# FFN gate and up: one 512-column product for both parts of x, halves added on VectorE, and GpSimd scaling x one instruction per tile

## The chip, the cores and the metric

The kernel runs on one core of one Trainium2 chip, as one launch. The metric is the device time of that launch in microseconds, the median of several runs. Each core has five engines that run their own instruction streams and meet at semaphores: TensorE (PE, matrix products; its weight loads are shown as PEld), VectorE (DVE), ScalarE (ACT), GpSimd (POOL), and SyncE (SP), which here issues the loads. A product reads a stationary operand of 128x128 and a moving one of up to 512 columns, and writes up to one PSUM bank (128 x 512 fp32). There are eight banks.

## The reference, cut to what matters

Two transformer blocks follow one another on 256 tokens of width 1024. The first has attention, retention, a memory attention and a mixture of 32 experts. The second has two layers, each with two feed-forward networks (FFN) around a mixer, so four FFN in all. Everything is fp32. The part that the change works on is this:

```python
D_MODEL = 1024; SEQ = 256; D_FF = 2816; DEPTH_2 = 2
def _swiglu(h, w_gu, w_down):
    gate, up = jnp.split(h @ w_gu, 2, axis=-1)
    return (jax.nn.silu(gate) * up) @ w_down
...
for l in range(DEPTH_2):
    x = _layer_norm(alpha * x + 0.5 * _swiglu(x, ffn_w_gu[l, 0], ffn_w_down[l, 0]), ln_g[l, 0], ln_b[l, 0])
    mix = _token_mixers(x, ...)
    x = _layer_norm(alpha * x + mix, ln_g[l, 1], ln_b[l, 1])
    x = _layer_norm(alpha * x + 0.5 * _swiglu(x, ffn_w_gu[l, 1], ffn_w_down[l, 1]), ln_g[l, 2], ln_b[l, 2])
```

`_layer_norm` ends in `* g + b`; that scaling of x is what GpSimd does in `pool_affine`. The first block's attention has 8 heads (`ATTN_HEADS`) and 4 retention heads.

## The kernel before, in words

**Split operands.** Products run in the rounded format fp32r. To keep fp32 accuracy, each operand is split in a high part (the rounded value) and a low part (the rest), and a product a*b becomes three: high*high, high*low, low*high. For the FFN, `whu` and `wlu` are the high and low part of a tile's gate and up weights, `whd` and `wld` those of its down weights, `xh` and `xl` those of x transposed (8 blocks `k` of 128 features by 256 tokens), `hh` and `hl` those of the hidden values.

**Tiles.** An FFN (numbered `g`, 0 to 3) has `FT` = 22 tiles `t` of 128 hidden units. Buffers alternate by `p` = t mod 2. For each tile PE does `up(t, p)` (L1031): for the two halves `m` (0 gate, 1 up) and the eight blocks `k`, three products of 256 columns, (`whu`,`xh`), (`whu`,`xl`), (`wlu`,`xh`), into columns `m*256` on of bank 4+p. Then `down(t, p)` (L1072): 12 products of 512 columns into banks 0 to 3, which hold the sum over all tiles. The order on PE is written out: `up_first()` (tile 0, L1050, the products with `xl` last, since `xl` comes later), then a loop of 20 rounds `up(t+1)`, `down(t)`, then `up(21)`, and at the end `down_into` (L1057) for tiles 20 and 21 by banks: nine products of tile 20, a wait for the hidden values of tile 21 (`f_h`), then three products for each bank of tile 21.

**The other engines.** ACT: `silu(t)` (L1106) reads the gate half of the bank into `sg`, then waits for the end of `down(t-1)` and makes `whd(t+1)` and `whu(t+2)` (`ffn_high`, L928). DVE: `hidden(t)` multiplies `sg` with the up half of the bank into `hf` (L1158), rounds it into `hh` (L1160) and subtracts for `hl` (L1162, which signals `f_h`); then `low(t+1)` and `low(t+2)` subtract for `wld(t+1)` and `wlu(t+2)` (`ffn_low`, L933, which counts up `wl_ok`). SP streams 1.5 MB per tile into a ring.

**GpSimd in an FFN.** `pool_affine` scales x with `ln`: four multiplications of 128x512 (L976), then four additions (L981). In FFN 1, 2 and 3 it starts when `wl_ok` shows that `wld` of tile 1 is made, and runs through. Its end (`xp_ok`) is waited for only before the next `ln` is loaded and in the norm after the FFN.

**The end of an FFN.** After `silu(21)` ACT makes the high part of the next stage's weights (L512, or L928 for the next FFN), POOL the low part (L521, or L939), then POOL the inverse root of the norm (L566), ACT scales x (L1214, L1215), and PE transposes (L1010).

**The attention of the first block** (about 97 to 134 us). `pe_units` walks over the 8 heads `u`. The table `AHEAD1` says in which step the scores (L1965) of which heads are computed: heads 0 and 1 in step 0, 2 and 3 in step 1, 4 and 5 in step 3, 6 and 7 in step 5. Head v's scores lie in bank v mod 2, so they wait until DVE has taken the logits of head v-2 (`lg_ok`). Between them stand retention scores (L2099) and values (L2110), transposes of probabilities (L1975) and attention values (L1984). DVE makes the logits (L2055) and their maxima (L2059) one head ahead, and the norm of retention (L2527, L2530, L2536, with POOL's L2120, L566 in between).

## Time and profile before

| | us |
|---|---|
| median of 3 runs | 1827.29 |
| lowest, highest run | 1823.26, 1829.07 |
| the profiled execution | 1831.82 |
| its span, first to last instruction | 1830.0 |
| PE busy in the span | 1645.0 (90%) |
| DVE busy | 853.7 (47%) |
| ACT busy | 639.8 (35%) |
| POOL busy | 262.6 (14%) |
| four FFN, about | 736 to 920, 1085 to 1268, 1281 to 1467, 1631 to 1819 |
| experts, about | 290 to 735 |

A row of the chain of work gives start, length, what ran and how many instructions. A matmul's recorded length includes its way through the array: the pace is the distance between starts, not the length. "waited for" and "idle before" name what released an engine.

### The profile page before, as it was taken

The page shows a single profiled execution, that of the slowest core. Times are in us where ns is not written, and L with a number is a line of the kernel's source. Part 1 is how long each engine was busy: PE and PEld are TensorE (multiplying, and loading weights), DVE is VectorE, ACT ScalarE, POOL GpSimd, SP SyncE. Part 2 cuts the span into 40 slices and gives each one's busy share as a digit, 9 for nine tenths or more (in the row PEclk, how much of TensorE's full clock was granted, in tenths as well). Part 3 has the DMA queues.
Part 4 walks back from the last instruction along what each step waited for, and adds up shares of the span by engine and source line. Part 5 has one row for each costly group of instructions (what it writes and reads, how often), then busy time and mean ns, then how long its engine had stood idle before and what let it go on. Part 6 is the DMA issues. An engine that isn't in the chain of part 4 may idle for free.

```text
span 1830.0 us, 29586 instructions
## 1 busy us (share of the span) xinstructions
PE 1645.0 (90%) x11837; PEld 1310.8 (72%) x11837; DVE 853.7 (47%) x1290; ACT 639.8 (35%) x948; POOL 262.6 (14%) x253
## 2 busy tenths in 40 slices
PE   8989999777766776999999899999999999899997
PEld 6777885333323332999977779998999977779996
DVE  4574443111110111555555655555655565666555
ACT  5445442100010011333433644444333333644442
POOL 1233210000000000100143422001300143431000
PEclk9989999977788887999999999999999999999999
DMA  9514578999999999945533054536454543055501
GB/s 393 171 38 138 195 283 334 425 426 427 426 426 426 425 426 407 358 176 188 198 138 138 24 198 180 185 124 236 176 194 180 187 149 124 24 207 182 196 35 46
DMA packets 60949, 421.38 MB, mean 230 GB/s; under 512 B 7008, under 2 KB 16064, under 8 KB 17216
## 3 DMA queue, kind: packets, MB, share of 16 engines
q1 hardware_dynamic: 59136, 409.13, 57.0%
q10 hardware_dynamic: 1728, 11.03, 1.7%
q8 instruction: 64, 1.05, 0.2%
q14 instruction: 21, 0.17, 0.0%
HBM read 419.08 MB, written 1.05 MB: 230 GB/s over the span
## 4 chain that ended last, share of the span: by engine, by line
PE 63%; DMA 10%; SPq 9%; DVE 5%; ACT 5%; POOL 4%; issue 4%; DVEq 0%; ACTq 0%; POOLq 0%
PE bank L1031 26%; PE bank L1072 12%; SPq L1683 9%; PE bank L1820 6%; PE bank L1771 5%; DMA ring<-in_we 4%; DMA more<-in_we 4%; PE bank L1846 2%; PE bank L650 2%; DMA ring<-in_wf 1%; PE bank L1984 1%; POOL small L566 1%; PE bank L1050 1%; PE bank L1965 1%; POOL wlu L939 1%
## 5 line engine op out<-in xcount | busy, mean ns | idle before, releaser
L1031 PE MATMUL bank<-xh,wlu 128*128 128x256 f32 x1344 | 379.9, 283 | 0.0
L1031 PE MATMUL bank<-xh,whu 128*128 128x256 f32 x1344 | 379.8, 283 | 0.0
L1031 PE MATMUL bank<-xl,whu 128*128 128x256 f32 x1344 | 379.8, 283 | 0.0
L1031 PEld LDWEIGHTS bank<-xh,whu 128*128 128x128 f32 x1344 | 257.0, 191 | 3.3
L1031 PEld LDWEIGHTS bank<-xl,whu 128*128 128x128 f32 x1344 | 256.9, 191 | 3.3
L1031 PEld LDWEIGHTS bank<-xh,wlu 128*128 128x128 f32 x1344 | 257.2, 191 | 0.0
L933 DVE TENSOR_TENSOR wlu<-ring,whu 128x2048 fp32r<-128x2048 f32 x84 | 196.3, 2337 | 51.2 <-ACT whu L928 51.2
L933 DVE TENSOR_TENSOR wld<-ring,whd 128x1024 fp32r<-128x1024 f32 x88 | 110.0, 1250 | 188.6 <-ACT whd L928 188.6
L928 ACT ACTIVATE whu<-ring 128x2048 fp32r (+1 forms) x88 | 167.2, 1902 | 3.5 <-DMA ring<-in_wf 3.5
L928 ACT ACTIVATE whd<-ring 128x1024 fp32r (+1 forms) x88 | 93.3, 1060 | 206.1 <-PE bank L1072 202.6
L650 PE MATMUL bank<-ring,xg 128*32 128x256 f32 x1424 | 104.0, 430 | 40.6 <-DMA ring<-in_we 40.6
L1820 PE MATMUL bank<-ring_r,xTh 128*128 128x512 f32 x384 | 112.9, 407 | 9.9 <-POOL ring_r L490 6.0
L1106 ACT ACTIVATE sg<-bank 128x256 f32<-128x256 f32 x88 | 33.8, 384 | 228.5 <-PE bank L1031 210.0
L939 POOL TENSOR_TENSOR wlu<-ring,whu 128x512 fp32r<-128x512 f32 x16 | 20.1, 1287 | 648.8 <-ACT whu L928 614.3
L650 PEld LDWEIGHTS bank<-ring,xg 128*32 128x32 f32 x1424 | 43.9, 119 | 96.1 <-DMA ring<-in_we 68.6
L669 PE MATMUL bank<-ring,hTe 128*32 128x256 f32 x832 | 75.6, 499 | 36.0 <-DMA ring<-in_we 27.6
L829 DVE TENSOR_TENSOR hmid<-hact,bank 128x128 f32<-128x128 f32 x32 | 9.2, 288 | 199.9 <-ACT hact L717 199.9
L1072 PE MATMUL bank<-whd,hl 128*128 128x512 f32 x320 | 100.9, 397 | 0.0
L1072 PE MATMUL bank<-whd,hh 128*128 128x512 f32 x320 | 100.5, 395 | 0.0
L1072 PE MATMUL bank<-wld,hh 128*128 128x512 f32 x320 | 100.4, 394 | 0.0
L1820 PEld LDWEIGHTS bank<-ring_r,xTh 128*128 128x128 f32 x384 | 73.5, 194 | 28.7 <-issue 8.8
L521 POOL TENSOR_TENSOR ring_r<-ring,high 128x512 fp32r<-128x512 f32 x32 | 41.3, 1322 | 349.2 <-ACT high L512 349.0
(317 smaller groups left out, 2745.6 us busy)
## 6 DMA issues: line engine op xcount, KB each, us to landing
ring<-in_we SPq DMA_DIRECT2D x141, 1024.0 KB, 26.8
ring<-in_wf SPq DMA_DIRECT2D x88, 1536.0 KB, 6.8
ring<-in_w SPq DMA_DIRECT2D x52, 1024.0 KB, 4.9
more<-in_we SPq DMA_DIRECT2D x51, 1024.0 KB, 25.7
ring<-in_w SPq DMA_DIRECT2D x32, 256.0 KB, 3.4
ln<-in_ln ACTq DMA_DIRECT2D x6, 1024.0 KB, 4.9
bias<-in_bias ACTq DMA_DIRECT2D x2, 2048.0 KB, 8.1
bias<-in_bias SPq DMA_DIRECT2D x1, 2048.0 KB, 20.1
```

The costliest lines, as they stand in the source:

```text
L521: ins = eng.tensor_tensor(slot_r[s][:, part], slot[s][:, part], run.highs[c % 2][:, part].bitcast(F32), ALU.subtract)
L650: ins = pe.matmul(bank[4 + e % 2][q * CAP:(q + 1) * CAP, 0:2 * P], xg[:, k, e * CAP:(e + 1) * CAP], w[:, kk, q], start=(k == 0), stop=(k = ...
L669: ins = pe.matmul(bank[6][q * CAP:(q + 1) * CAP, 0:2 * P], hTe[:, e % 2, k * CAP:(k + 1) * CAP], w[:, kk, q], start=(k == 0), stop=(k == 3 ...
L928: act.activation(dst[:], ring[:, bass.ds(ring_tile(t) + first, D if down else 2 * D)], ACT.Copy).then_inc(wh_ok, 1)
L933: eng.tensor_tensor(dst[:], ring[:, bass.ds(ring_tile(t) + first, D if down else 2 * D)], src[:].bitcast(F32), ALU.subtract).then_inc(done, 1)
L939: ins = eng.tensor_tensor(wlu[p][:, c0:c0 + 512], ring[:, ring_tile(t) + c0:ring_tile(t) + c0 + 512], whu[p][:, c0:c0 + 512].bitcast(F32), ...
L1031: ins = pe.matmul(bank[4 + p][:, m * S:(m + 1) * S], w[p][:, cols], v[:, k], start=(k == 0 and n == 0), stop=(k == KD - 1 and n == 2))
L1072: ins = pe.matmul(bank[2 * i + c][:], v[p][:, tok(i)], w[p][:, c * 512:(c + 1) * 512], start=False, stop=False, skip_group_check=True)
L1683: sp.dma_start(slot[s], src).then_inc(e_land[s], 16)
L1771: ins = pe.matmul(bank[sel + 2 * i + c0 // 512][:, 0:c1 - c0], v[:, k, tok(i)], w[:, kk, c0:c1], start=(k == 0 and m == 0), stop=(k == KD ...
L1820: ins = pe.matmul(bank[banks[2 * i + h]][:], v[:, k, tok(i)], w[:, kk, h * 512:(h + 1) * 512], start=(k == 0 and m == 0), stop=(k == KD - ...
L1846: ins = pe.matmul(bank[b][:, i * MD:(i + 1) * MD], v[:, k, tok(i)], w[:, k], start=(k == 0 and m == 0), stop=(k == KD - 1 and m == 2))
```

## The change

**Products.** `xh` and `xl` become the two halves of one tile `xhl`. In `up`, the two products with `whu` become one of 512 columns whose moving operand is `xhl[:, :, k]`, two runs of 256 columns that lie 2048 elements apart. The product with `wlu` stays at 256 columns and adds into the first half. Gate now has a bank of its own (4 + 2p) and up another (5 + 2p); in each bank the first half holds the products with `xh`, the second that with `xl`. `up_first` keeps 48 products of 256 columns, with `xl` into the second half.

**Halves.** `hidden` begins with two `tensor_reduce` instructions on DVE, which read a whole bank and add the halves: gate into `sg` (signals `f_ga`), up into `hf`. ACT's `silu` waits for `f_ga` in place of `f_gu` and works on `sg` in place; the multiplication reads `sg` and `hf`, both in SBUF.

**GpSimd.** In FFN 1 to 3 `pool_affine` starts one count of `wl_ok` later (`wlu` of tile 2 is made) and then waits two counts, that is one tile, before each further instruction.

**Attention.** `AHEAD1` now computes the scores of one head per step: after heads 0 and 1 in step 0, head u+1 in step u.

```diff
-        xh = at("xh", work + 12288, [P, KD, S], F32R)
-        xl = at("xl", work + 20480, [P, KD, S], F32R)
+        xhl = at("xhl", work + 12288, [P, 2, KD, S], F32R)
+        xh, xl = xhl[:, 0], xhl[:, 1]
...
-        AHEAD1 = {0: (0, 1), 1: (2, 3), 3: (4, 5), 5: (6, 7)}
+        AHEAD1 = {0: (0, 1), **{u: (u + 1,) for u in range(1, AH - 1)}}
...
-        def pool_affine(pool, st, j, after):
-
-            pool.wait_ge(*after)
+        def pool_affine(pool, st, j, after, step=0):
+
+            sem_at, first = after
+            pool.wait_ge(sem_at, first)
...
+            for n in range(8):
+                i, c = n // 2 % 2, n % 2
+                cols = slice(c * 512, (c + 1) * 512)
+                if n == 4:
+                    st.sync()
+                if n and step:
+                    pool.wait_ge(sem_at, first + n * step)
+                ins = pool.tensor_tensor(x[:, i, cols], x[:, i, cols], ln[:, n // 4, cols], (ALU.mult, ALU.add)[n // 4])
+                if n < 7:
+                    st.then(ins)
...
-                        for n, (w, v) in enumerate(((whu, xh), (whu, xl), (wlu, xh))):
-                            ins = pe.matmul(bank[4 + p][:, m * S:(m + 1) * S], w[p][:, cols], v[:, k],
-                                            start=(k == 0 and n == 0), stop=(k == KD - 1 and n == 2))
+                        into = bank[4 + 2 * p + m]
+                        pe.matmul(into[:].rearrange("p (a s) -> p a s", a=2), whu[p][:, cols], xhl[:, :, k],
+                                  start=(k == 0), stop=False, skip_group_check=True)
+                        ins = pe.matmul(into[:, 0:S], wlu[p][:, cols], xh[:, k],
+                                        start=False, stop=(k == KD - 1), skip_group_check=True)
...
+                        if g == 0 and m == 1 and not low_x:
+                            pe.wait_ge(t_out, tb + 2)
...
-                act.wait_ge(f_gu, t + (g * FT + 1))
-                act.activation(sg[:, p], bank[4 + p][:, 0:S], ACT.Silu).then_inc(f_sg, 1)
+                act.wait_ge(f_ga, t + (g * FT + 1))
+                act.activation(sg[:, p], sg[:, p], ACT.Silu).then_inc(f_sg, 1)
...
+                gate, upper = bank[4 + 2 * p], bank[5 + 2 * p]
+                dve.wait_ge(f_gu, t + (g * FT + 1))
+                dve.tensor_reduce(sg[:, p], gate[:].rearrange("p (a s) -> p s a", a=2), X, ALU.add).then_inc(f_ga, 1)
+                dve.tensor_reduce(hf[:, p], upper[:].rearrange("p (a s) -> p s a", a=2), X, ALU.add).then_inc(f_hv, 1)
                 dve.wait_ge(f_sg, t + (g * FT + 1))
-                dve.tensor_tensor(hf[:, p], sg[:, p], bank[4 + p][:, S:2 * S], ALU.mult).then_inc(f_hv, 1)
-                dve.wait_ge(f_hv, t * 2 + (g * FT * 2 + 1))
+                dve.wait_ge(f_hv, t * 3 + (g * FT * 3 + 1))
+                dve.tensor_tensor(hf[:, p], sg[:, p], hf[:, p], ALU.mult).then_inc(f_hv, 1)
...
-                    pool_affine(pool, st, l * 3 - 1, (wl_ok, (g + 1) * FFN_W + 4))
+                    pool_affine(pool, st, l * 3 - 1, (wl_ok, (g + 1) * FFN_W + 5), 2)
...
-                pool_affine(pool, st, l * 3 + 1, (wl_ok, (g + 1) * FFN_W + 4))
+                pool_affine(pool, st, l * 3 + 1, (wl_ok, (g + 1) * FFN_W + 5), 2)
```

The order of instructions at two places. First PE in the attention of the first block, in steps 3 and 4: L1965 (after: L1975) are scores, with bank0 for an even head and bank1 for an odd one, L2110 (L2120) retention values, L1984 (L1994) attention values, L1975 (L1985) transposes, L2099 (L2109) retention scores. Before:

```order
L1975 MATMUL bank2<-ident_53,lg1_143 128x128 x4
L1965 MATMUL bank0<-qkT_94 128x256
L1965 MATMUL bank1<-qkT_94 128x256
L1965 MATMUL bank0<-qkT_94 128x256
L1965 MATMUL bank1<-qkT_94 128x256
L2110 MATMUL bank7<-proj_92,xT_51 128x128 x4
L1984 MATMUL bank4<-proj_92,xT_51 128x64 x4
L1975 MATMUL bank3<-ident_53,lg1_143 128x128 x4
L2099 MATMUL bank6<-qkT_94 128x256 x2
```

The same place of PE with the change:

```order
L1985 MATMUL bank2<-ident_53,lg1_142 128x128 x4
L1975 MATMUL bank0<-qkT_94 128x256 x2
L2120 MATMUL bank7<-proj_92,xT_51 128x128 x4
L1994 MATMUL bank4<-proj_92,xT_51 128x64 x4
L1985 MATMUL bank3<-ident_53,lg1_142 128x128 x4
L1975 MATMUL bank1<-qkT_94 128x256 x2
L2109 MATMUL bank6<-qkT_94 128x256 x2
```

Head 4's two score products now stand alone before the retention values, and head 5's have moved behind the next transposes, ahead of the retention scores.

Second, DVE at the start of the FFN loop: `hidden(0)`, then `wld` and `wlu`. Before, with what each instruction waits for:

```order
L1158 TENSOR_TENSOR hf<-sg,bank 128x256 [waits f_sg]
L1159 ISA
L1160 CAST hh_127<-hf 128x256 [waits f_hv]
L1161 REGISTER_ALU
L1162 TENSOR_TENSOR hl_129<-hf,hh_127 128x256 [waits f_hv]
...
L933 ISA [waits wh_ok]
L933 TENSOR_TENSOR wld_123<-ring,whd_119 128x1024
...
L933 TENSOR_TENSOR wlu_120<-ring,whu_116 128x2048
```

The same place of DVE with the change:

```order
L1164 TENSOR_REDUCE sg<-bank 128x256 [waits f_gu]
L1165 TENSOR_REDUCE hf<-bank 128x256
L1167 ISA [waits f_sg]
L1168 TENSOR_TENSOR hf<-sg,hf 128x256 [waits f_hv]
L1169 REGISTER_ALU
L1170 CAST hh_126<-hf 128x256 [waits f_hv]
L1171 REGISTER_ALU
L1172 TENSOR_TENSOR hl_128<-hf,hh_126 128x256 [waits f_hv]
...
L934 TENSOR_TENSOR wld_123<-ring,whd_119 128x1024
...
L934 TENSOR_TENSOR wlu_120<-ring,whu_116 128x2048
```

Two reductions now stand ahead of the multiplication, and DVE, not ACT, is the first to wait for PE.

## Rows read from the trace of the kernel before

**Rows 1.** The page: granted clock of PE in 40 slices, tenths of full.

```profile
PEclk9989999977788887999999999999999999999999
```

**Rows 2.** The page: the chain that ended last, by line, shares of the span.

```profile
PE bank L1031 26%; PE bank L1072 12%; SPq L1683 9%; PE bank L1820 6%; PE bank L1771 5%; DMA ring<-in_we 4%; DMA more<-in_we 4%; PE bank L1846 2%; PE bank L650 2%; DMA ring<-in_wf 1%; PE bank L1984 1%; POOL small L566 1%; PE bank L1050 1%; PE bank L1965 1%; POOL wlu L939 1%
```

**Rows 3.** The chain in order of time, in FFN 0: start, length, what.

```profile
750.52 5.75 PE bank L1031 x48
756.27 2.80 PE bank L1072 x12
```

**Rows 4.** Stretch of FFN 0: length, busy PE, PEld, DVE, ACT, POOL; clock, DMA share, GB/s.

```profile
760.00:900.00 140.00, 140.00 (x990) 131.36 (x989) 76.72 (x82) 54.10 (x50) 0.00 (x0) 1.00 0.53 195
```

**Rows 5.** PE in order of time, in a mixer: 512 columns, then 160.

```profile
980.90 0.39 PE L1771 MATMUL bank<-high,xl 128*128 128x512 f32 x1
981.13 0.24 PE L1771 MATMUL bank<-high,xTh 128*128 128x160 f32 x1
981.21 0.27 PE L1771 MATMUL bank<-ring_r,xTh 128*128 128x160 f32 x1
981.32 0.28 PE L1771 MATMUL bank<-high,xl 128*128 128x160 f32 x1
```

**Rows 6.** The chain before FFN 1: four bf16 products of 512 columns.

```profile
1079.61 0.86 PE bank L991 x4
```

**Rows 7.** Groups of 760 to 900 us: count, busy, mean ns, idle before, releaser.

```profile
L933 DVE TENSOR_TENSOR wlu<-ring,whu 128x2048 fp32r<-128x2048 f32 x17 | 39.0, 2293 | 9.9 <-ACT whu L928 9.9
...
L933 DVE TENSOR_TENSOR wld<-ring,whd 128x1024 fp32r<-128x1024 f32 x17 | 20.8, 1226 | 43.3 <-ACT whd L928 43.3
...
L1162 DVE TENSOR_TENSOR hl<-hf,hh 128x256 fp32r<-128x256 f32 x16 | 6.8, 426 | 0.5
L1158 DVE TENSOR_TENSOR hf<-sg,bank 128x256 f32<-128x256 f32 x16 | 6.7, 421 | 11.1 <-ACT sg L1106 11.1
L1106 ACT ACTIVATE sg<-bank 128x256 f32<-128x256 f32 x16 | 6.1, 384 | 44.2 <-PE bank L1031 44.2
L1160 DVE CAST hh<-hf 128x256 fp32r<-128x256 f32 x16 | 4.7, 293 | 0.5
```

**Rows 8.** DVE reductions by shape, whole span; columns as in Rows 7.

```profile
L2052 DVE TENSOR_REDUCE small<-bank 128x2 f32<-128x512 f32 x16 | 11.0, 690 | 5.5 <-PE bank L1965 4.4 <-PE bank L1975 0.9
...
L2458 DVE TENSOR_REDUCE small<-tmp 128x16 f32<-128x1024 f32 x2 | 2.4, 1220 | 0.1
```

**Rows 9.** DVE in order of time: a reduction and the instruction behind it.

```profile
97.99 0.69 DVE L2059 TENSOR_REDUCE small<-lg 128x2 f32<-128x512 f32 x1
98.60 0.68 DVE L2055 SCALAR_TENSOR_TENSOR lg<-bank,bias 128x512 f32<-128x512 f32 x1
```

**Rows 10.** The chain in order of time, at the end of FFN 0.

```profile
918.69 0.02 ACT sg L1106
...
920.96 5.00 POOL ring_r L521 x4
```

**Rows 11.** The chain in order of time, at the end of FFN 3.

```profile
1812.63 2.82 PE bank L1057 x12
```

**Rows 12.** DVE in order of time, the same place, tile 21.

```profile
1813.87 0.43 DVE L1162 TENSOR_TENSOR hl<-hf,hh 128x256 fp32r<-128x256 f32 x1
```

**Rows 13.** DVE in FFN 2 while POOL scales x, tile 1.

```profile
1294.52 0.41 DVE L1158 TENSOR_TENSOR hf<-sg,bank 128x256 f32<-128x256 f32 x1
1294.96 0.94 DVE L1160 CAST hh<-hf 128x256 fp32r<-128x256 f32 x1
1295.94 1.40 DVE L1162 TENSOR_TENSOR hl<-hf,hh 128x256 fp32r<-128x256 f32 x1
```

**Rows 14.** PE in the first attention: the scores of heads 4 and 5.

```profile
108.28 2.08 PE L1965 MATMUL bank<-qkT 64*128 64x256 f32 x8
```

**Rows 15.** DVE in the first attention: the logits of head 4.

```profile
110.39 0.69 DVE L2055 SCALAR_TENSOR_TENSOR lg<-bank,bias 128x512 f32<-128x512 f32 x1 [0.73 <-PE bank L1965]
```

**Rows 16.** A stretch of the first attention, columns as in Rows 4.

```profile
124.00:130.00 6.00, 5.74 (x28) 5.54 (x29) 2.92 (x11) 2.21 (x7) 1.90 (x3) 0.57 0.01 3
```

19 lines of the change are left out of this document (5 added, 14 removed).

## The prediction

> **What bounds the kernel now.** I read the page from the top. The chain that ended last, by line, gives the FFN products most: L1031 (gate and up) 26% and L1072 (down) 12% of the span [rows 2]. The experts' stage in the middle, where the clock row dips to 7 [rows 1], hangs on loads (L1683 and the two DMA entries, together 17% [rows 2]); the change does not enter it. Then I read the chain in order of time inside an FFN: 5.75 us of L1031, 2.80 us of L1072, and again, 8.55 us a tile with nothing between [rows 3]. The stretch from 760 to 900 us confirms it: PE busy 140.00 of 140.00 us at full clock (2.4 GHz), DVE only 76.72, ACT 54.10 [rows 4]. So in the loops PE alone sets the pace. Last, the two places where a loop's end hands over to other engines, and the first attention, since the change touches both.
>
> **The products.** The loop's pace gives the prices. 48 products of 256 columns take 5.75 us, 119.8 ns each; 12 of 512 columns take 2.80 us, 233.3 ns each [rows 3]. At 2.4 GHz the columns alone are 106.7 and 213.3 ns, so what comes on top is 13.1 ns for a short product and 20.0 ns for a long one. Each block k now has one long and one short product: 233.3 + 119.8 = 353.1 ns in place of 3 x 119.8 = 359.4, 6.3 ns less. A tile has 16 such blocks, 0.10 us; 21 tiles in each of four FFN go through `up` (tile 0 goes through `up_first`, whose count stays), 84 x 16 x 6.3 ns = 8.5 us off the path that sets the end. This is small because the number of columns stays the same; only the number of instructions falls.
>
> Two things in that price are not shown by any row. First, a moving operand in two runs: it could cost nothing, or as much as two products, 2 x 119.8 = 239.6 ns, which leaves no gain. I take nothing, since a run that continues 8 KB further on is still one instruction with one weight load. Second, the mixture: in a run of their own 160-column products follow each other at 0.11 us, though their columns need 0.067, so there the weight load sets the pace; but the first one, right behind a long product, gives way after 0.08 us [rows 5]. So behind a long product the next weights are ready early. If part of the 13.1 ns is such a wait, the short product could fall to about 109 ns, 10.8 x 1344 = 14.5 us more gain. Against it: the long product, whose load is surely covered, has 20 ns on top. I keep 119.8, and the other as the lower end.
>
> Four bf16 products of 512 columns take 0.86 us, 215 ns each [rows 6]: in that format 1.7 ns come on top, in fp32r 20. So most of the surcharge is not one per instruction, and a reading by which only about 2 ns are saved per product left out is a rival below. The Trainium skill (TensorE: Matmul & The Clock Gate, Wait — 56ns, not 53.3ns?) gives a warm gap of the columns' time plus 2.5 ns; by it 2.5 x 1344 = 3.4 us would be gained. This trace's 119.8 ns disagrees with it, its 215 ns agrees.
>
> **The halves, inside the loop.** A reduction of 512 elements from a bank takes 0.69 us; one of 1024 elements into 16 outputs 1.22, so the price goes by elements read, not by outputs [rows 8]. The next instruction starts 0.61 us after it [rows 9]. Two per tile add 1.2 us to DVE's 76.72 / 16.4 = 4.7 us per tile (140 us are 16.4 tiles) [rows 4]: 5.9 of 8.45. The order matters too. `hidden(t)` grows from 0.4 (silu) + 1.2 to about 2.6 us, and what comes behind it in DVE's queue is `wld(t+1)`, which today waits 43.3 / 17 = 2.5 us per tile for ACT, since ACT makes `whd` only after `down(t-1)` [rows 7]. So 1 us more fits in. PE wants `hl(t)` only after `up(t+1)`, 5.65 us after `up(t)` ended. ACT's `silu` starts 0.7 us later and has 44.2 / 16 = 2.8 us of idle time before it [rows 7]. Cost inside the loop: nothing, in any tile.
>
> **GpSimd.** While POOL scales x, DVE's cast takes 0.94 and its subtraction 1.40 us in place of 0.29 and 0.43; the multiplication, with one input in PSUM, stays at 0.41 [rows 7, 13]. PE does not wait even so. The Trainium skill (SBUF — State Buffer, Who interferes with whom) says that GpSimd blocks a DVE instruction with both inputs in SBUF but never a reduction. The rows agree for the subtraction; no row shows a reduction beside POOL. The new multiplication has both inputs in SBUF, so it joins those that are held up. Spread over tiles, each POOL instruction starts when `wlu` is done, and its 1.25 us (four take 5.00 [rows 10]) lie beside the reductions. Either way the hold-ups, at most three times 1 us, stay below the 3 us that `hidden` may grow further. Eight instructions end at tile 10 of 22, and nothing waits for them before tile 20. Queued behind the waiting POOL is only work of the FFN's end. Zero.
>
> **The ends of the FFN.** Here no next tile covers DVE. With U the end of `up(21)`: before, `silu` starts at U + 0.02, and ACT's next work, then POOL's 5.00 us, hang on it [rows 10]. After, the gate reduction runs from U + 0.04 to U + 0.73, `silu` starts at U + 0.76 and, from SBUF, may take 0.03 longer: 0.75 us later on the chain, at the end of FFN 0, 1 and 2 (the same pattern stands in the chain after FFN 1 and 2): 2.25 us. At the end of FFN 3 there is no POOL work; there PE is next. Before, `hl(21)` is done at 1813.87 + 0.43 = 1814.30, U + 1.67 [rows 12], while PE has nine products of 233.3 ns first, U + 2.10 [rows 11]: spare 0.43. After: reductions until U + 1.34, multiplication at 1.37, cast 0.45 later, subtraction 0.33 later and 0.43 long: U + 2.6. PE waits 0.5 us. Together 2.75 us of loss.
>
> `up_first`'s new wait in FFN 0 is for `xl` of the second of four pairs of blocks, and PE computes 16 products, 1.9 us, ahead of it. At worst it is one DVE instruction of 512 elements late, 0.69 us [rows 15], once; I take zero. The new banks 6 and 7 are free by then in each FFN.
>
> **The attention.** DVE waits 0.73 us for the scores of head 4 [rows 15], since PE computes those of heads 4 and 5 interleaved in 2.08 us [rows 14]. Head 4 alone takes half, 1.0 us less, and the retention values behind it come 1.0 us earlier too. So 0.7 us fall away. The later steps hang on DVE and POOL, not on PE, and head 5's scores, now behind the next transposes, still come 1 us before DVE wants them. The rest of the kernel follows: SP loads experts only once the attention gives slots free. But the clock there is in question: it was at 0.57 from 124 to 130 us [rows 16], and PE's runs of 1.2 GHz may move. I keep 0.7 us, with 2 us either way.
>
> **The sum.** -8.5 + 2.75 - 0.7 = -6.4 us. Against the profiled execution: 1831.8 becomes 1825.4. That run lay 4.5 us above the median of the runs shown, so the median becomes 1827.3 - 6.4, about 1821 us.
>
> **Rivals.**
> (a) The products gain nothing: the two runs cost as two products. The losses at the ends remain: -0.7 + 2.75 = +2 us, 1829. For it: no row has such an operand. Close to it, only some 2 ns are saved per product: 1344 x 2 = 2.7, net -0.6, 1827. Chance of the two 0.2.
> (b) The short product gets cheaper beside a long one: -6.4 - 14.5 at most, 1806; half of it 1814. For it: the 0.08 us [rows 5]. Chance 0.13.
> (c) Slower: DVE becomes the bound, because a reduction over pairs pays per output. It decides from 8.45 - 4.7 = 3.75 us for the two, 1.9 each, three times the price taken. If each took as long as the 2048-element subtraction, 2.2 us of pace [rows 7], a tile would take 4.7 + 4.4 = 9.1 us, 0.65 x 84 = 55 us more: 1880. Against it: 16 outputs cost no more than 2 per element [rows 8]. Half-way, at 1.2 us each, the loop still hides it and the ends lose 3 us more: 1824. Chance of slower by this 0.03.
> (d) The attention meets the low clock at a worse moment, or the two-run product is dearer than two (from 242 ns on the kernel loses over 0.3%): 1833. Chance 0.04.
>
> **How the numbers follow.** The forecast, 1821, has 0.6; its own range is 1817 to 1825. The range for 8 in 10 reaches down into (b) and up to (a): 1811 to 1829. The bound of 0.3% (5.5 us, about what a measurement of this kernel tells from no change) lies at 1821.8, just beside the forecast: of its 0.6 some 0.37 are faster, and with (b) 0.5. Same: 0.23 + 0.2 + 0.01 = 0.44. Slower: 0.06.
>
> **What would show it.** In the profile after: `up` of a tile at 5.65 us in place of 5.75, and `down` at 2.80. Starts of long and short products 0.233 and 0.120 us apart: if 0.24, (a); if 0.11, (b). The reductions at 0.69 us and no wait of PE in the stretch of FFN 0. `silu(21)` 0.75 us after PE's end, a PE wait of 0.5 us in L1057's last part, and no wait for L1965 before head 4's logits. Wrong it would be if a POOL instruction, once released late, still ran at the FFN's end, or if PE waited for `f_h` in the loop.

## The result, and the profile after

The changed kernel takes 1814.05 us, median of 9 runs (1810.24 to 1820.49), against 1827.29 us for the kernel before in the same session (1823.26 to 1832.12, 9 runs). The ratio is 0.9923, with a 95% interval of 0.9907 to 0.9938: 13.2 us faster, where 6.4 us had been forecast. The direction was right and 1814 lies inside the range of 1811 to 1829, but below the forecast's own 1817 to 1825: the size is twice that of the sum, so a term of it is wrong or one is missing.

The page of the changed kernel, its head, the granted clock and the chain that ended last by line (to hold against [rows 1, 2]):

```profile
span 1811.9 us, 27202 instructions
...
PE 1628.0 (90%) x10493; PEld 1230.8 (68%) x10493; DVE 953.7 (53%) x1466; ACT 643.3 (36%) x948; POOL 247.3 (14%) x253
...
PEclk9999999878867887999999999999999999999998
...
PE bank L1032 17%; PE bank L1077 12%; SPq L1693 9%; DMA ring<-in_we 9%; PE bank L1034 9%; PE bank L1830 6%; PE bank L1781 5%; PE bank L1856 2%; DMA more<-in_we 2%; DMA ring<-in_wf 1%; PE bank L651 1%; PE bank L1994 1%; POOL small L567 1%; PE bank L1975 1%; PE bank L1055 1%
```

L1032 is now the 512-column product of gate and up, L1034 the 256-column one; together they hold the place that L1031 had. The span fell from 1830.0 to 1811.9 us, 18.1 us and thus more than the medians differ. The chain in order of time tells why at once: it enters FFN 0's first products, up_first, at 731.10 us (the first of them starts at 730.75), and did so at 735.97 before, and at that point not a single changed product has run.

The chain of the changed kernel in order of time in FFN 0, the products of down alone (start, length, what):

```profile
742.50 2.80 PE bank L1077 x12
...
750.86 2.81 PE bank L1077 x12
...
759.32 2.81 PE bank L1077 x12
```

From one `down` to the next it is 8.36 us, then 8.46, then 8.36 again: the pace before was 8.55 [rows 3]. So `up` of a tile takes 5.55 us in every second tile and 5.65 in the others; 5.65 was the forecast for all. TensorE in order of time, in an even tile and in the odd one behind it (start, duration, line, tiles, shape):

```profile
747.23 0.39 PE L1032 MATMUL bank<-xhl,whu 128*128 128x512 f32 x1
747.46 0.28 PE L1034 MATMUL bank<-xhl,wlu 128*128 128x256 f32 x1
747.58 0.39 PE L1032 MATMUL bank<-xhl,whu 128*128 128x512 f32 x1
...
747.92 0.39 PE L1032 MATMUL bank<-xhl,whu 128*128 128x512 f32 x1
...
755.62 0.40 PE L1032 MATMUL bank<-xhl,whu 128*128 128x512 f32 x1
755.86 0.28 PE L1034 MATMUL bank<-xhl,wlu 128*128 128x256 f32 x1
755.97 0.40 PE L1032 MATMUL bank<-xhl,whu 128*128 128x512 f32 x1
...
756.32 0.40 PE L1032 MATMUL bank<-xhl,whu 128*128 128x512 f32 x1
```

The durations overlap, so the starts are what to read. Two blocks of the even tile take 747.92 - 747.23 = 0.69 us, two of the odd one 756.32 - 755.62 = 0.70. Over all starts of FFN 0 the mean distance behind a long product is 235.8 ns in odd tiles and 231.5 in even ones, behind a short one 117.0 and 115.4: a block of 352.8 ns (forecast 353.1) or 346.9. Before, the mean was 119.5 to 119.9 ns in both kinds of tile. These means hide a cycle: from tile 3 on the distances of an odd tile repeat every three blocks (232.5, 117.5, 240.8, 120.0, 235.8, 113.4 ns), those of an even one every two (232.5, 117.5, 230.8, 112.5). Before, the first eight products behind `down` took 116.6 to 120.9 ns, 118.0 on the mean, and all behind them 120.0.

The stretch from 760 to 900 us (columns as in rows 4), and VectorE in one tile of it (in brackets its idle time ahead of the instruction, and what ended it):

```profile
760.00:900.00 140.00, 140.00 (x735) 118.82 (x734) 98.46 (x119) 56.30 (x52) 0.00 (x0) 1.00 0.53 196
```

```profile
759.35 0.69 DVE L1164 TENSOR_REDUCE sg<-bank 128x256 f32<-128x512 f32 x1 [0.15 <-PE bank L1034]
759.96 0.68 DVE L1165 TENSOR_REDUCE hf<-bank 128x256 f32<-128x512 f32 x1
760.68 0.42 DVE L1168 TENSOR_TENSOR hf<-sg,hf 128x256 f32<-128x256 f32 x1
761.13 0.29 DVE L1170 CAST hh<-hf 128x256 fp32r<-128x256 f32 x1
761.46 0.43 DVE L1172 TENSOR_TENSOR hl<-hf,hh 128x256 fp32r<-128x256 f32 x1
763.47 1.23 DVE L934 TENSOR_TENSOR wld<-ring,whd 128x1024 fp32r<-128x1024 f32 x1 [1.58 <-ACT whd L929]
```

TensorE still never waits; VectorE has risen from 76.72 to 98.46 us and still waits 1.58 us for ScalarE ahead of `wld`. The reductions cost 0.69 us each although they write 256 outputs from pairs: the price goes by elements read.

At the ends the tile has no cover. ScalarE behind the last tile of FFN 0, and the last tile of FFN 3 on TensorE and VectorE:

```profile
911.34 0.42 ACT L1111 ACTIVATE sg<-sg 128x256 f32<-128x256 f32 x1 [5.31 <-DVE sg L1164]
911.66 1.90 ACT L513 ACTIVATE high<-ring 128x2048 fp32r<-128x2048 f32 x1
```

```profile
1793.50 0.39 PE L1062 MATMUL bank<-whd,hh 128*128 128x512 f32 x1
1793.70 0.69 DVE L1164 TENSOR_REDUCE sg<-bank 128x256 f32<-128x512 f32 x1 [3.32 <-PE bank L1034]
...
1795.88 0.42 DVE L1172 TENSOR_TENSOR hl<-hf,hh 128x256 fp32r<-128x256 f32 x1
1796.36 0.50 PE L1062 MATMUL bank<-whd,hh 128*128 128x512 f32 x1 [0.59 <-DVE hl L1172]
```

SiLU is now released by the reduction, and TensorE waits 0.59 us for `hl` in the tail, forecast 0.5.

To compare kernels without the chance of their first 730 us, I cut each trace by the same marks. "Loop" is from the first product of `down` to the last product of `up` in an FFN; "end" from the last product of `up` of FFN 0 or 2 to the first product with `high`; "FFN 1 to 2" from the last of `up` to the first of `down`; "tail" from the last of `up` to the last instruction; "mixer" from the first product with `high` to the next FFN's first product. All in us, from starts to starts:

| kernel | FFN 0 starts | each loop | end 0, end 2 | FFN 1 to 2 | tail | mixer 1, 2 |
|---|---|---|---|---|---|---|
| before | 736.0 | 170.8 | 13.55, 13.56 | 27.81 | 17.64 | 150.5, 150.5 |
| changed | 730.7 | 168.0 | 14.34, 14.33 | 27.22 | 18.49 | 148.9, 148.9 |

The mixers' instructions are the same in both kernels. Their 1.5 us come from the granted clock. A stretch of the first mixer, 43 us behind its start in both (columns as in rows 4), before and after:

```profile
975.00:985.00 10.00, 10.00 (x56) 8.65 (x56) 1.93 (x3) 1.39 (x3) 6.72 (x11) 0.84 0.26 90
```

```profile
968.00:978.00 10.00, 10.00 (x72) 9.18 (x71) 1.85 (x4) 1.39 (x3) 6.46 (x11) 1.00 0.43 156
```

TensorE is busy all the time in both, but the clock is 0.84 of full on the mean before (3.2 us of this stretch lie at 0.50) and 1.00 after. The same product, the 181st of the mixer, starts 46.4 us behind the mixer's start before and 44.9 after, and from there on the 1.6 us stay. The counts, 56 and 72, differ by more than the clock, since the stretches end among products of other widths. The same happens once more between FFN 1 and FFN 2, where the kernel before computes its first products like this:

```profile
1282.00:1285.00 3.00, 3.00 (x15) 2.71 (x14) 3.00 (x6) 0.00 (x0) 0.00 (x0) 0.50 0.00 0
```

Clock 0.50 is the lower of the two levels, 1.2 GHz. The changed kernel has 1.00 in the stretch that answers to it.

### The profile page after: what moved, and what is told of

It reads as the page before. It is cut to its first block, busy times and chain, and to the rows that moved or that the text cites. A ratio compares the mean times of both kernels' runs of the same rounds, so it can differ in the third digit from the quotient of the medians.

```text
span 1811.9 us, 27202 instructions
## 1 busy us (share of the span) xinstructions
PE 1628.0 (90%) x10493; PEld 1230.8 (68%) x10493; DVE 953.7 (53%) x1466; ACT 643.3 (36%) x948; POOL 247.3 (14%) x253
## 4 chain that ended last, share of the span: by engine, by line
PE 61%; DMA 12%; SPq 10%; ACT 5%; DVE 4%; POOL 4%; issue 4%; DVEq 0%; ACTq 0%; POOLq 0%
PE bank L1032 17%; PE bank L1077 12%; SPq L1693 9%; DMA ring<-in_we 9%; PE bank L1034 9%; PE bank L1830 6%; PE bank L1781 5%; PE bank L1856 2%; DMA more<-in_we 2%; DMA ring<-in_wf 1%; PE bank L651 1%; PE bank L1994 1%; POOL small L567 1%; PE bank L1975 1%; PE bank L1055 1%
## 5 line engine op out<-in xcount | busy, mean ns | idle before, releaser
L1032 PE MATMUL bank<-xhl,whu 128*128 128x512 f32 x1344 | 474.2, 396 | 0.0
L1034 PE MATMUL bank<-xhl,wlu 128*128 128x256 f32 x1344 | 375.3, 279 | 0.0
L1032 PEld LDWEIGHTS bank<-xhl,whu 128*128 128x128 f32 x1344 | 252.3, 188 | 60.6
L1034 PEld LDWEIGHTS bank<-xhl,wlu 128*128 128x128 f32 x1344 | 253.2, 188 | 3.5
L934 DVE TENSOR_TENSOR wlu<-ring,whu 128x2048 fp32r<-128x2048 f32 x84 | 192.6, 2293 | 51.4 <-ACT whu L929 51.4
L1111 ACT ACTIVATE sg<-sg 128x256 f32<-128x256 f32 x88 | 36.9, 419 | 278.8 <-DVE sg L1164 278.8
L651 PEld LDWEIGHTS bank<-ring,xg 128*32 128x32 f32 x1424 | 44.9, 122 | 94.9 <-DMA ring<-in_we 65.7
L670 PE MATMUL bank<-ring,hTe 128*32 128x256 f32 x832 | 71.9, 478 | 37.5 <-DMA ring<-in_we 28.0
L1077 PE MATMUL bank<-whd,hh 128*128 128x512 f32 x320 | 100.5, 395 | 0.0
L695 DVE COPY yg<-bank 32x256 f32<-32x256 f32 x64 | 27.1, 424 | 124.5 <-PE bank L670 124.0
L982 POOL TENSOR_TENSOR x<-x,ln 128x512 f32<-128x512 f32 x40 | 59.4, 1497 | 212.8 <-DVE wlu L934 198.4
L483 ACT ACTIVATE ring_r<-ring 128x2048 fp32r<-128x2048 f32 x32 | 61.5, 1921 | 61.5 <-PE bank L1830 57.7
```

The source lines that it names most:

```text
L483: act.activation(high1[n % 2], slot[n % SLOTS1], ACT.Copy).then_inc(dh_ok, 1)
L651: ins = pe.matmul(bank[4 + e % 2][q * CAP:(q + 1) * CAP, 0:2 * P], xg[:, k, e * CAP:(e + 1) * CAP], w[:, kk, q], start=(k == 0), stop=(k = ...
L670: ins = pe.matmul(bank[6][q * CAP:(q + 1) * CAP, 0:2 * P], hTe[:, e % 2, k * CAP:(k + 1) * CAP], w[:, kk, q], start=(k == 0), stop=(k == 3 ...
L934: eng.tensor_tensor(dst[:], ring[:, bass.ds(ring_tile(t) + first, D if down else 2 * D)], src[:].bitcast(F32), ALU.subtract).then_inc(done, 1)
L982: ins = pool.tensor_tensor(x[:, i, cols], x[:, i, cols], ln[:, n // 4, cols], (ALU.mult, ALU.add)[n // 4])
L1032: pe.matmul(into[:].rearrange("p (a s) -> p a s", a=2), whu[p][:, cols], xhl[:, :, k], start=(k == 0), stop=False, skip_group_check=True)
```

## The experiments

Each ran beside the kernel before on the same chip, in four sessions; a ratio is to the kernel before in the same session, and there is one trace of each kernel. The theory to test: the loop's gain is the merging of two products into one and nothing else; the ends lose 0.8 us each to the reductions; the order of scores and GpSimd's spreading are worth about nothing; the rest of the 13.2 us is clock.

**The attention's order alone.** The kernel before, with the order of the changed one:

```diff
-        AHEAD1 = {0: (0, 1), 1: (2, 3), 3: (4, 5), 5: (6, 7)}
+        AHEAD1 = {0: (0, 1), **{u: (u + 1,) for u in range(1, AH - 1)}}
```

> The kernel before with only the new order of the scores in the first attention (head u+1 one ahead, not in pairs). Theory A (the order removes the one wait of 0.73 us and no more, as predicted): 1826.5 us, 0.7 under the kernel before, ratio 0.9996, and the start of FFN 0 0.7 us earlier in the trace. Rival B (the earlier work changes what clock the tensor engine is granted in the attention and the dense stretch behind it; between the two traces FFN 0 starts 4.9 us earlier, 735.97 against 731.10): 1823 us, ratio 0.9977, with FFN 0 starting near 731. Rival C (nothing): 1827.3.

Measured: 1826.22 us against 1826.46 for the kernel before, ratio 1.0005 (0.9987 to 1.0023). FFN 0 started at 728.8 us in its trace. **And its opposite**, the changed kernel with the old order:

> The changed kernel with the old order of the scores in the first attention. Theory A: 0.7 us slower than the changed kernel's 1814.05, so 1814.8. Rival B (the clock follows the order): 1818 us, with FFN 0 starting near 736. Rival C: 1814.

Measured: 1813.97 us, ratio 0.9940 (0.9923 to 0.9957), FFN 0 at 730.0. The runs show no effect of the order: with it alone the ratio is 1.0005, and without it the changed kernel's is 0.9940 for 0.9923, with intervals that overlap. So rival B falls, and 0.7 us can't be told from 0, since each ratio is uncertain by 3 us. The start of FFN 0 is no measure of it either: in the fourteen traces of this study it lies between 728.2 and 739.1 us, with no relation to the order. One cause shows in the stretch from 112 to 150 us, in the order_alone run and in the last_early run (below), whose first 700 us are written alike. TensorE's half clock begins at 100.5 us in the one and lasts 3.4 us; in the other it begins at 100.8 and lasts 20.5:

```profile
112.00:150.00 38.00, 35.61 (x222) 30.48 (x219) 24.52 (x52) 18.89 (x44) 10.85 (x12) 1.00 0.23 75
```

```profile
112.00:150.00 38.00, 35.85 (x208) 30.66 (x208) 22.16 (x55) 18.69 (x48) 10.09 (x11) 0.83 0.08 28
```

So the 5 us by which FFN 0 starts earlier in the changed kernel's trace lie within what runs of such kernels differ by, and they make most of the step from the medians' 13.2 to the spans' 18.1 us.

**Three products in the new banks.** The changed kernel with the merge undone:

```diff
-                        pe.matmul(into[:].rearrange("p (a s) -> p a s", a=2), whu[p][:, cols], xhl[:, :, k],
-                                  start=(k == 0), stop=False, skip_group_check=True)
+                        pe.matmul(into[:, 0:S], whu[p][:, cols], xh[:, k], start=(k == 0), stop=False, skip_group_check=True)
+                        pe.matmul(into[:, S:2 * S], whu[p][:, cols], xl[:, k], start=False, stop=False, skip_group_check=True)
```

> The changed kernel, but the steady products of gate and up are again three of 256 columns for each block k (W_high x_high and W_low x_high into the left half, W_high x_low into the right half of the bank); banks, reductions, order and GpSimd's instructions stay as changed. Theory A (the whole gain of the loop is the merging of two products into one of two runs): the pitches are 119.8 ns, up 5.75 us again, and the kernel 12 us slower than the changed one: 1826. Rival B (part of the 12 us comes from the banks, gate and up now being in different ones): pitches below 119.8 ns in it, 1818 to 1823 us. Rival C (the reductions on VectorE delay the tensor engine): a wait of the tensor engine in the loop; over 1828.

Measured: 1824.60 us, ratio 1.0000 (0.9979 to 1.0021), 10.6 us above the changed kernel by the medians and 14 by the ratios. Its products stand 119.6 to 119.8 ns apart in both kinds of tile, each loop takes 170.8 us again, ends, tail and FFN 1 to 2 are those of the changed kernel (14.33, 14.32, 18.49, 27.33), and TensorE does not wait in the loops. Theory A holds: the merge makes the whole difference of the loops, 11.8 us, and the banks and reductions give the tensor engine nothing.

**One run in place of two.** The long product reads and writes 512 columns in a row, so that the kernel adds up other products and only its time counts:

```diff
-                        pe.matmul(into[:].rearrange("p (a s) -> p a s", a=2), whu[p][:, cols], xhl[:, :, k],
+                        pe.matmul(into[:], whu[p][:, cols], xhl[:].rearrange("p a k s -> p (a k s)")[:, k * 2 * S:(k + 1) * 2 * S],
```

> The changed kernel, but the 512-column product of gate and up reads 512 columns that stand in a row (2k and 2k+1 of the flat x_high, x_low) and writes the whole bank in one run, so it computes other sums. Theory A (a product of two runs costs what one of one run costs): same time as the changed kernel, 1814, and pitches of 236 or 231 ns in the two parities of tile again. Rival B (the two runs cost something, or the gap between the two parities comes from them): the pitch falls to 230 in both parities, (236 - 231) x 16 blocks x 42 tiles = 3.4 us under, 1810.5.

Measured: 1812.61 us, ratio 0.9917 (0.9895 to 0.9940), and exactly the changed kernel's distances, 235.8 and 117.0 in odd tiles, 231.5 and 115.4 in even ones, loops of 168.0 us. An operand in two runs costs what one in one run costs. Rival (a) of the prediction is dead, and the two paces do not come from the operand.

**The other order within a block.** The 256-column product first:

```diff
-                        pe.matmul(into[:].rearrange("p (a s) -> p a s", a=2), whu[p][:, cols], xhl[:, :, k],
-                                  start=(k == 0), stop=False, skip_group_check=True)
-                        ins = pe.matmul(into[:, 0:S], wlu[p][:, cols], xh[:, k],
-                                        start=False, stop=(k == KD - 1), skip_group_check=True)
+                        pe.matmul(into[:, 0:S], wlu[p][:, cols], xh[:, k],
+                                  start=(k == 0), stop=False, skip_group_check=True)
+                        ins = pe.matmul(into[:].rearrange("p (a s) -> p a s", a=2), whu[p][:, cols], xhl[:, :, k],
+                                        start=False, stop=(k == KD - 1), skip_group_check=True)
```

> The changed kernel with the two products of each block k in the other order: the 256-column one (W_low x_high) ahead of the 512-column one. Theory A (each product pays its own columns and 13 to 20 ns, whatever stands ahead of it): the block takes 347 or 353 ns by parity as in the changed kernel, 1814. Rival B (a short product is cheaper behind a long one, whose columns hide the load of its weights, and the next long one then pays): the split between the two moves while the sum stays. Rival C (the order matters for the sum): a block of 359 ns, 1823, or one of 340, 1809.

Measured: 1813.53 us, ratio 0.9924 (0.9905 to 0.9943); behind a short product 116.8 and 115.0 ns, behind a long one 236.4 and 231.6. Neither the split nor the sum moves. But this run can't decide what I made it for: in either order long and short products alternate, and a short one stands behind a long one in both. So it shows that the order within a block costs nothing, and leaves rival (b)'s mechanism, a short product that is cheaper behind a long one, untested. Its size is refuted by the changed kernel itself: the short product fell by 2.8 and 4.4 ns, not by 10.8. Its direction has something for it in three_products, where the first short product behind `down` takes 116.7 ns and those behind the eighth 120.0.

**Where the two paces come from.** Three runs, each with one of these edits, moved things between even and odd tiles: the banks (the first four lines and the like in the reductions), the two buffers of the low weights, the two of the high ones.

```diff
-                        into = bank[4 + 2 * p + m]
+                        into = bank[6 - 2 * p + m]
...
+                else:
+                    pe.wait_ge(xh_ok, xb + 4)
...
-        wlu = [at("wlu0", work + 53248, [P, CH], F32R), at("wlu1", work + 45056, [P, CH], F32R)]
+        wlu = [at("wlu0", work + 45056, [P, CH], F32R), at("wlu1", work + 53248, [P, CH], F32R)]
...
-        whu = [at("whu0", work, [P, CH], F32R), at("whu1", work + 28672, [P, CH], F32R)]
+        whu = [at("whu0", work + 28672, [P, CH], F32R), at("whu1", work, [P, CH], F32R)]
```

> The changed kernel with gate and up of the even tiles in banks 6 and 7 and of the odd tiles in banks 4 and 5 (the first products of an FFN then wait for all four parts of x, up to 1.5 us at each FFN). In the changed kernel the products of the odd tiles take 5.62 us and of the even ones 5.53. Theory A (the parity follows the bank that is written): odd tiles 5.53, even tiles 5.62. Rival B (it follows the weight buffers or the work of the other engines beside it): odd tiles 5.62 and even ones 5.53 as before. Time 1814 to 1820 in either case.

> The changed kernel with the two buffers of W_low (wlu0, wlu1) in each other's place in SBUF, nothing else. In the changed kernel a block k takes 236 + 117 ns in odd tiles and 231.5 + 115.4 in even ones, whichever banks are written. Theory A (the parity follows the place of W_low): even tiles now take the longer ones, 5.53 us in the loop and odd ones 5.43 (start of the first to start of the last product). Rival B (it follows the place of W_high, or the other engines' work, or the code): odd tiles 5.53, even ones 5.43 as before. The time is 1814 in either case.

> The changed kernel with the two buffers of W_high of gate and up (whu0, whu1) in each other's place in SBUF, nothing else. Theory A (the parity follows the place of W_high): even tiles 5.53 us, odd ones 5.43. Rival B (neither the place of W_low nor that of W_high: the other engines' work or the code): odd tiles 5.53 and even ones 5.43. The time is 1814 in either case.

Measured: in all three the odd tiles take 5.53 us from the first to the last start and the even ones 5.43, as in the changed kernel. Neither the banks nor the place of one pair of buffers decides; a last run (mirrored_early, below) moved both pairs at once, with the same outcome. The tile's number does not decide either, as the pool_undone run (next) shows: in FFN 1 TensorE waits once, ahead of tile 3, and from tile 4 to the end it is the even tiles that take 5.53 us and the odd ones 5.43. `down` of tiles 2 to 5 in the chain of that run:

```profile
1104.12 2.81 PE bank L1077 x12
...
1112.57 2.81 PE bank L1077 x12
...
1120.93 2.81 PE bank L1077 x12
...
1129.38 2.81 PE bank L1077 x12
```

From one to the next these are 8.45, 8.36 and 8.45 us; at the same tiles the changed kernel has 8.36, 8.45 and 8.36. In FFN 2 and 3 a wait of the same length did not exchange the two. The cycles of distances thus depend on what ran and waited before; what sets them stays open.

Times: low_swapped 1811.57 us, ratio 0.9907 (0.9890 to 0.9925); high_swapped 1814.45, 0.9938 (0.9918 to 0.9959). The banks' swap cost far more than I expected: 1825.67 us, ratio 1.0001 (0.9984 to 1.0018), because the first products then wait for all of x. FFN 1 to 2 takes 30.15 us in place of 27.22, each mixer with the wait at its end 151.6 in place of 148.9. Together with a slower start of FFN 1 and 3 this is 10.4 us in the traces from FFN 0 on (11.6 by the medians), for one late start at three places. Much of it may be clock: 17 us more than in the changed kernel lie at 0.50 there, which can cost half of that, 8.5 us, at most (an estimate).

**GpSimd in one go.** The changed kernel with the old `pool_affine`: four multiplications and four additions in a row.

```diff
-            for n in range(8):
-                i, c = n // 2 % 2, n % 2
-                cols = slice(c * 512, (c + 1) * 512)
-                if n == 4:
-                    st.sync()
-                if n and step:
-                    pool.wait_ge(sem_at, first + n * step)
...
+            for i in range(NT):
+                for c in range(2):
+                    cols = slice(c * 512, (c + 1) * 512)
+                    st.then(pool.tensor_tensor(x[:, i, cols], x[:, i, cols], ln[:, 0, cols], ALU.mult))
```

> The changed kernel with GpSimd's eight instructions on x in one go again instead of one for each tile. Theory A (they are off the path, and the tensor engine does not wait for the VectorE work that they slow, as predicted: 0): 1814 us, and no wait of the tensor engine in the first tiles of FFN 1 to 3. Rival B (with the two reductions VectorE has less slack, and two or more instructions of GpSimd beside one tile, where a multiply took 1.18 us for 0.43, push the hidden vector past the products of up): waits of 1 to 3 us in tiles 2 to 5 of FFN 1 to 3, up to 1820.

Measured: 1819.68 us, ratio 0.9958 (0.9944 to 0.9972): 5.6 us slower than the changed kernel, and the intervals of the two ratios do not meet. The group of products in this run (columns: count, busy, mean ns, then the idle time of the engine ahead of them, and what ended it), then TensorE's own waits from 1075 to 1251 us, which is FFN 1:

```profile
L1032 PE MATMUL bank<-xhl,whu 128*128 128x512 f32 x1344 | 474.4, 396 | 4.5 <-DVE wlu L934 4.5
```

```profile
PE bank L1032 <- DVE wlu L934: 1.5, 1, 1.5
```

The same 1.5 us stand in FFN 2 and FFN 3. GpSimd, VectorE and the product that waits, in order of time:

```profile
1083.77 7.28 POOL L977 TENSOR_TENSOR x<-x,ln 128x512 f32<-128x512 f32 x4 [14.52 <-DVE wld L934]
...
1087.13 0.68 DVE L1164 TENSOR_REDUCE sg<-bank 128x256 f32<-128x512 f32 x1
...
1088.44 1.46 DVE L1168 TENSOR_TENSOR hf<-sg,hf 128x256 f32<-128x256 f32 x1
...
1089.93 1.27 DVE L1170 CAST hh<-hf 128x256 fp32r<-128x256 f32 x1
...
1091.13 8.27 POOL L982 TENSOR_TENSOR x<-x,ln 128x512 f32<-128x512 f32 x4
1091.23 1.48 DVE L1172 TENSOR_TENSOR hl<-hf,hh 128x256 fp32r<-128x256 f32 x1
...
1092.63 2.31 DVE L934 TENSOR_TENSOR wld<-ring,whd 128x1024 fp32r<-128x1024 f32 x1
...
1094.87 3.38 DVE L934 TENSOR_TENSOR wlu<-ring,whu 128x2048 fp32r<-128x2048 f32 x1
...
1098.30 0.50 PE L1032 MATMUL bank<-xhl,whu 128*128 128x512 f32 x1 [1.50 <-DVE wlu L934]
```

In one tile beside GpSimd, the multiplication takes 1.46 us for 0.42, the cast 1.27 for 0.29, the subtraction 1.48 for 0.43, `wld` 2.31 for 1.23 and `wlu` 3.38 for 2.29: 5.2 us more in a tile of 8.4, in which VectorE had 5.9 us of work. The reduction alone stays at 0.68. In the changed kernel GpSimd's one instruction of a tile falls just on the two reductions (1094.84 to 1096.13 us), takes 1.29 us and holds up nothing; the multiplication at 1096.17 takes its 0.42:

```profile
1094.82 1.29 POOL L982 TENSOR_TENSOR x<-x,ln 128x512 f32<-128x512 f32 x1 [6.23 <-DVE wlu L934]
```

In pool_undone `wlu` comes too late for the next products, once in each of FFN 1 to 3. The loops of these took 169.64, 169.75 and 169.75 us in place of 167.96, together 5.3 us, nearly the whole 5.6; FFN 0, where GpSimd scales nothing, stayed at 167.96. The Trainium skill (SBUF — State Buffer, Who interferes with whom) says that a VectorE instruction with two SBUF inputs contends with GpSimd's reads, that a cast can, and that a reduction never does on this chip. The rows agree on all three: 1.46, 1.27 and 0.68.

**The last tile in the old form.** The changed kernel, but tile 21 of each FFN with three products for each block, gate and up summed in banks 6 and 7, SiLU from the bank:

```diff
-            up(FT - 1, 1)
+            up_last()
...
-            silu(FT - 1, 1)
+            act.wait_ge(f_gu, (g + 1) * FT)
+            act.activation(sg[:, 1], bank[6][:, 0:S], ACT.Silu).then_inc(f_sg, 1)
...
-            hidden(FT - 1, 1)
+            dve.tensor_tensor(hf[:, 1], sg[:, 1], bank[7][:, 0:S], ALU.mult).then_inc(f_hv, 1)
```

> The changed kernel, but tile 21 of each FFN is computed in the old form: three products of 256 columns for each block k, gate summed in one bank and up in the next, SiLU reading the bank, no reductions. Theory A (the reduction ahead of SiLU costs 0.80 us at the end of each FFN, of which the longer up of this tile, 0.10 to 0.19 us, is given back): 0.6 x 4 = 2.4 us under the changed kernel, 1811.6 us; the ends of FFN 0 and FFN 2 last 13.3 us again from the last product of up, not 14.06. Rival B (the end is held by another thing, the down products or GpSimd): 1814.

Measured: 1811.82 us, ratio 0.9935 (0.9910 to 0.9959). The cuts of its trace show the mechanism to the tenth: end 13.58 and 13.58, FFN 1 to 2 26.48, tail 17.61, loops 168.07. Against the changed kernel that is 0.75 us twice, 0.74 and 0.88 less, and 0.44 more for the longer products: 2.7 us. But its mixers took 150.5 us each, 1.6 us more than in the changed kernel's trace, and the granted clock of the stretch 43 us behind the mixer's start is this:

```profile
964.00:974.00 10.00, 10.00 (x55) 8.67 (x53) 2.37 (x3) 1.40 (x3) 7.19 (x11) 0.84 0.22 71
```

That is the picture of the kernel before, with its clock of 0.84. **With SiLU still earlier**, released when the gate half is done:

```diff
+                    ins.then_inc((f_gl, f_gu)[m], 1)
...
+            act.wait_ge(f_gl, g + 1)
+            act.activation(sg[:, 1], bank[6][:, 0:S], ACT.Silu).then_inc(f_sg, 1)
```

> The changed kernel with tile 21 of each FFN in the old form (as in last_old) and its SiLU released when the gate half is done, so that it runs beside the products of the up half. Theory A (SiLU of 0.39 us and its start stand on the path at the end of each FFN): 0.3 to 0.5 us for each FFN under last_old, where FFN 0 and 2 are held by ScalarE's copy behind SiLU and FFN 1 and 3 by the products of down behind the hidden vector; 1810.2 us, ends of FFN 0 and 2 12.9 us in place of 13.3. Rival B (the end is held by another wait): 1811.8 as last_old. Both beat the kernel before and the changed kernel.

Measured: 1814.00 us, ratio 0.9925 (0.9906 to 0.9944). Ends 13.32 and 13.31, FFN 1 to 2 26.20, tail 17.64: another 0.26 to 0.28 us at each of the first three (0.3 to 0.5 had been expected), nothing in the tail, where TensorE still has products of tile 20 to do. The sum of these cuts is 3.5 us under the changed kernel. The chain behind the last product of FFN 0 no longer has SiLU in it:

```profile
914.92 3.97 PE bank L1045 x33
...
918.92 1.93 ACT high L514
...
920.92 5.03 POOL ring_r L523 x4
```

**The same with the buffers mirrored.** The lines of `wlu` and `whu` as above at once, and the places of the two `wld`, `hh` and `hl` exchanged in the same way:

> The kernel last_early (tile 21 in the old form, its SiLU released after the gate half) with both buffers of W_high and of W_low of gate and up, those of W_low of down and those of the hidden vector's two parts in each other's place in SBUF. It is also the second look at the fastest form. Theory A on the two speeds of products (they come from a combination of places in SBUF): even tiles 5.53 us and odd ones 5.43. Rival B (they come from the order of the code, or from something no view shows): odd 5.53 and even 5.43, as in every kernel so far. On the ends: FFN 1's first product of up to FFN 2's takes 194.3 us (changed kernel 195.2), and the last FFN's to the last VectorE work on x 187.7 (188.5), so about 0.8 to 0.9 for each of the four ends and 3 us in all: 1811.

Measured: 1814.64 us, ratio 0.9927 (0.9907 to 0.9948). Odd tiles 5.53, even 5.43, so these places in SBUF do not decide together either. Ends 13.31 and 13.30, FFN 1 to 2 26.18, tail 17.62.

So the shorter ends are real at their place, and the median does not show them: 1811.8, 1814.0 and 1814.6 against 1814.05, ratios 0.9925 to 0.9935 against 0.9923, all intervals overlapping. All three beat the kernel before; that one of them beats the changed kernel is not shown. The mixers' column tells where it may have gone:

| ends | first mixer | second mixer |
|---|---|---|
| short (before, order_alone, last_old, last_early, mirrored_early) | 150.5 in all five | 150.5 in three, 147.6 in two |
| long (changed, order_undone, pool_undone, one_run, short_first, low_swapped, high_swapped) | 146.0 to 148.9 | 146.0 to 148.9 |

With the long ends the mixers' mean is 148.0 us, with the short ones 149.9. (three_products had 150.3 and 146.0 with long ends, so the ends alone do not fix it; banks_swapped is left out, as its mixers hold its wait.) Nor does the timing ahead of a mixer: changed, one_run, low_swapped and high_swapped have loops and ends alike to 0.02 us, and mixers of 146.0, 147.3 and 148.9 us. What fixes a mixer's length in every trace is how much of it lies at 0.50: none gives 146.0 us, 3.4 us give 147.2 to 147.7, 6.8 give 148.9 and 10.2 give 150.3 to 150.5. With one trace of each kernel, what is chance from run to run and what comes from the kernel can't be told apart.

## Why the prediction was right in direction and half in size

Put together for the two profiled kernels: loops 11.8 us less (2.85 each by the cut, and 0.10 for `up(1)` ahead of it), ends 0.79 + 0.77 more, tail 0.85 more, FFN 1 to 2 0.49 less without `up(1)`'s 0.10, mixers 3.1 less. That is -13.0 (from FFN 0's first product to the end the two traces differ by 12.9), beside the medians' -13.2. Of this, -8.7 is what the edits do (loops -11.8, ends +3.15, FFN 1's included), and -4.3 is clock: the mixers' 3.1 and 1.2 between FFN 1 and FFN 2. That the clock of one trace each fills the rest so closely is partly luck.

**What bounds the kernel: right.** TensorE sets the pace of the loops before and after, and a gain in its products comes through in full.

**The products, -8.5 us: mechanism right, size wrong; measured -11.8.** The block at 353.1 ns was right for the odd tiles (352.8). In even tiles it is 346.9, 12.5 ns under the old 359.4 in place of 6.3. The term that failed is "I keep 119.8": the short product fell to 117.0 and 115.4 ns, and the long one, which I had taken as 233.3 from `down`, is 235.8 or 231.5. What I had read as the price of a product in fp32r was the price in one sequence, not of the instruction. Rival (b) had said that it could fall, to 109 ns at most, and had 1814 for half of that; the measured median is the same number, but with less from the products and 4.3 us from the clock, so that is luck. Whether its reason, the long product ahead, is behind the smaller fall was not tested. The trace of before had a hint that I did not read: where `up` follows `down`, 256 columns behind 512, its first products take 116.6 ns and not 120.0. What makes every second tile faster stays open.

**The halves inside the loop, 0: right.** Reductions of 0.69 us, TensorE busy 140.00 of 140.00 us, and three_products shows no wait in the loops.

**The ends, +2.75 us: each step right, the sum 3.15.** FFN 0 and 2 lost 0.79 and 0.77 (forecast 0.75), the tail 0.85 with a wait of 0.59 (forecast 0.5), and last_old takes back 0.76, 0.74, 0.75 and 0.88, FFN 1's 0.74 among them. Between FFN 1 and 2 the loss is hidden: the changed kernel is 0.49 us quicker there, since the stretch at half clock fell away. three_products, with the same ends and no stretch at half clock there, agrees: 27.33 against 27.81.

**GpSimd, 0: the number right, one of its two reasons wrong.** "Either way the hold-ups, at most three times 1 us, stay below the 3 us" is false for the eight in one go. It was true before: there the eight in one go made VectorE's work in tile 1 of FFN 1 2.4 us longer, and TensorE did not wait. With the edit VectorE has the reductions, 1.2 us more in a tile, and its multiplication, now with both inputs in SBUF, is held up as well, by 1.0 us. So the eight instructions in one go cost 5.6 us; the spreading is what keeps that away. The step that carries the zero is another one, "lie beside the reductions", and it was right: 1.29 us for the 1.25 that I had taken from GpSimd's work on weights, against 1.8 and 2.1 for each of the eight in a row. I had counted three hold-ups of 1 us and left out that `wld` and `wlu` behind them are held up as well, by 1.1 us each. The worth of the edit to GpSimd is to be read against the kernel that has the other edits in it, not against the kernel before.

**The attention, -0.7 us: the wait was the clock's, not the order's.** In the changed kernel the logits of head 4 stand without a wait, as was said:

```profile
110.47 0.68 DVE L2065 SCALAR_TENSOR_TENSOR lg<-bank,bias 128x512 f32<-128x512 f32 x1
```

But they do so with the old order too. The 2.08 us of head 4's and 5's scores [rows 14], from which I took half, fell in a stretch at 0.50. That stretch before, and the scores of heads 6 and 7 behind it, at full clock:

```profile
107.70:111.10 3.40, 3.40 (x16) 2.24 (x15) 2.58 (x6) 2.71 (x4) 0.00 (x0) 0.50 0.00 0
```

```profile
116.91 1.14 PE L1965 MATMUL bank<-qkT 64*128 64x256 f32 x8
```

In order_undone, which has the old order, the half clock lies from 115.6 to 119.0 us. The scores of heads 4 and 5 take 1.13 us there, head 4's logits do not wait, and head 6's wait 0.71 us:

```profile
109.59 0.68 DVE L2065 SCALAR_TENSOR_TENSOR lg<-bank,bias 128x512 f32<-128x512 f32 x1
...
118.26 0.69 DVE L2065 SCALAR_TENSOR_TENSOR lg<-bank,bias 128x512 f32<-128x512 f32 x1 [0.71 <-PE bank L1975]
```

And in high_swapped, which has the new order and its half clock from 107.9 us on, head 4's logits wait 0.91 us for their scores. So the term took a wait that the clock makes for one that the order makes. From the attention's first product on `qkT` to the transposes of its result it took 43.3 us with the old order (order_undone) and 42.9 with the new. In the kernel before, with 10.2 us at half clock in it [rows 16], it was 46.5, and in the other traces with the new order 42.3 to 51.5, by where the half clock lay. The order's own part is some 0.4 us at most, and nothing by the medians.

**What was missing: the clock in the mixers.** The sum priced the clock in the attention alone, with 2 us either way. The mixers, which the change does not touch, gave 3.1 us between the two traces. They had stretches at 0.50: 10.2 us in each mixer before, 6.8 us in each after, and from 0 to 10.2 in the other runs. That the change of the end's length, 0.8 us, is what moved them is argued from the table of mixers and not shown, and the four kernels with like ends and unlike mixers speak against its being the only cause.

**The rivals.** (a) fell with one_run and the distances; (b) is as above, its size refuted and its mechanism untested; (c) did not come near: 0.69 us a reduction against 1.9. (d) did not happen in the changed kernel's trace, but its mechanism did in one_run, last_early and mirrored_early, all with the new order: 20.5 us at half clock in the attention, which took 51.5, 51.5 and 49.6 us. Whether the old order meets this less often can't be read from its two traces.
